# Plain fp32 on four column strips in place of split fp32r products, in the expert layer of a two-layer decoder trunk

## The reference, cut to what matters

```
D_MODEL, SEQ, N_EXPERTS, TOP_K_EXPERTS, D_FF_EXPERT = 1024, 256, 8, 2, 3584
def swiglu(h, w1, w3, w2):
    return (jax.nn.silu(h @ w1) * (h @ w3)) @ w2
def moe_ffn(h, router_w, w1, w3, w2):
    logits = (h @ router_w).astype(jnp.float32)
    vals, idx = lax.top_k(logits, TOP_K_EXPERTS)
    probs = jax.nn.softmax(vals, axis=-1)
    gate = jnp.sum(jax.nn.one_hot(idx, N_EXPERTS) * probs[..., None], axis=-2)
    out = jnp.zeros_like(h)
    for e in range(N_EXPERTS):
        out = out + gate[..., e:e + 1] * swiglu(h, w1[e], w3[e], w2[e])
    return out
```

## Time and profile before

| | |
|---|---|
| three runs | 1673.94, 1678.23, 1680.12 us; median 1678.23 us |
| the profiled execution | 1676.77 us, of which the span from first to last instruction is 1675.0 us |
| mean granted PE clock | 0.993 |
| busy share of the span | PE 98%, PEld 83%, DVE 81%, ACT 64%, POOL 27% |
| moved by DMA | 481.57 MB, of them 336 transfers of 1024 KB of expert weights |

### The profile page before, as it was taken

How to read it: one execution, slowest core, us unless ns; L and a number is a source line. 1 busy time by engine, 2 the same in 40 slices (tenths; PEclk the granted TensorE clock), 3 DMA queues, 4 the chain that set the end, 5 groups by cost and what they waited for, 6 DMA issues and landing times.

```text
span 1675.0 us, 24200 instructions
## 1 busy us (share of the span) xinstructions
PE 1641.8 (98%) x8916; PEld 1384.0 (83%) x8916; DVE 1363.3 (81%) x1134; ACT 1064.2 (64%) x894; POOL 444.8 (27%) x541
## 2 busy tenths in 40 slices
PE   8999999999999999999999999999999999999998
PEld 5887888999888788878888888888888888888886
DVE  5799675556669876688888988888888988888888
ACT  4345456444455544577777777777777777777775
POOL 8966802999152341233000000000000000000200
PEclk9999999999999999999999999999999999999999
DMA  8443556556445355389999999999999999999995
GB/s 294 158 158 115 175 189 217 181 190 219 150 152 176 126 176 185 121 314 396 384 381 388 365 384 385 367 386 385 369 387 382 372 384 377 379 383 370 391 395 195
DMA packets 212459, 481.57 MB, mean 287 GB/s; under 512 B 7936, under 2 KB 32640, under 8 KB 212144
## 3 DMA queue, kind: packets, MB, share of 16 engines
q1 hardware_dynamic: 207456, 463.34, 76.8%
q0 software_dynamic: 4512, 16.78, 2.7%
q10 hardware_dynamic: 432, 0.65, 0.1%
HBM read 473.40 MB, written 7.34 MB: 287 GB/s over the span
## 4 chain that ended last, share of the span: by engine, by line
PE 67%; DVE 2%; ACT 1%; issue 0%; DVEq 0%; ACTq 0%
PE ps L655 20%; PE ps L657 20%; PE ps L656 20%; PE ps L1330 1%; PE ps L701 1%; PE ps L703 1%; PE ps L702 1%; DVE w_lo L286 1%; PE ps L891 0%; PE ps L1406 0%; PE ps L1283 0%; ACT w_hi L280 0%; PE ps L1387 0%; DVE keybias L2171 0%; DVE keybias L2169 0%
## 5 line engine op out<-in xcount | busy, mean ns | idle before, releaser
L286 DVE TENSOR_TENSOR w_lo<-raw,w_hi 128x2048 fp32r<-128x2048 f32 (+1 forms) x433 | 1005.9, 2326 | 220.6 <-ACT w_hi L280 219.1
L280 ACT ACTIVATE w_hi<-raw 128x2048 fp32r<-128x2048 f32 (+1 forms) x433 | 830.0, 1918 | 410.1 <-PE ps L657 323.0
L655 PE MATMUL ps<-w_hi,xg_hi 128*128 128x512 f32 x896 | 354.5, 396 | 1.2 <-DVE w_lo L286 1.2
L657 PE MATMUL ps<-w_hi,xg_lo 128*128 128x512 f32 x896 | 349.5, 390 | 0.0
L656 PE MATMUL ps<-w_lo,xg_hi 128*128 128x512 f32 x896 | 349.0, 390 | 0.0
L655 PE MATMUL ps<-w_hi,hidT_hi 128*128 128x512 f32 x520 | 203.2, 391 | 0.0
L656 PE MATMUL ps<-w_lo,hidT_hi 128*128 128x512 f32 x520 | 202.5, 389 | 0.0
L657 PE MATMUL ps<-w_hi,hidT_lo 128*128 128x512 f32 x520 | 202.4, 389 | 0.0
L657 PEld LDWEIGHTS ps<-w_hi,xg_lo 128*128 128x128 f32 x896 | 168.2, 188 | 35.8
L655 PEld LDWEIGHTS ps<-w_hi,xg_hi 128*128 128x128 f32 x896 | 168.3, 188 | 35.4 <-DVE w_lo L286 1.7
L656 PEld LDWEIGHTS ps<-w_lo,xg_hi 128*128 128x128 f32 x896 | 168.5, 188 | 33.4
(11 more groups left out here) (432 smaller groups left out, 2409.5 us busy)
## 6 DMA issues: line engine op xcount, KB each, us to landing
raw<-moe_w SPq DMA_DIRECT2D x336, 1024.0 KB, 6.2
raw<-w_in SPq DMA_DIRECT2D x44, 1024.0 KB, 5.5
raw<-ffn_w SPq DMA_DIRECT2D x33, 1024.0 KB, 5.4
raw<-w_o SPq DMA_DIRECT2D x8, 1024.0 KB, 5.0
raw<-w_out_a SPq DMA_DIRECT2D x4, 1024.0 KB, 5.3
raw<-w_out_c SPq DMA_DIRECT2D x4, 1024.0 KB, 5.2
raw<-w_out_b SPq DMA_DIRECT2D x4, 1024.0 KB, 5.1
raw<-w_in SPq DMA_DIRECT2D x4, 904.0 KB, 7.4
```

The lines of the kernel that those rows point to most:

```text
L280: act.activation(w_hi[:, n % SPLIT, 0:width], raw[:, n % RAW, 0:width], ACT.Copy)\
L286: dve.tensor_tensor(w_lo[:, n % SPLIT, 0:width], raw[:, n % RAW, 0:width], w_hi[:, n % SPLIT, 0:width].bitcast(F32), ALU.subtract)\
L655: pe.matmul(dst, x_hi, hi, start=first, stop=False, skip_group_check=True)
L657: return pe.matmul(dst, x_lo, hi, start=False, stop=last, skip_group_check=True)
```

## The change

The expert layer and the router stop splitting. The experts multiply the raw chunks in plain fp32. `SLOTS` falls from 128 to 96 (up to three rounds would be made for fuller experts; the fullest has 71 tokens). The 96 slots are three strips of 32; each strip multiplies the first 384 of the 512 weight columns (`wide`). The fourth strip takes the last 128 columns for all three groups of slots, one after another (`narrow`), the first of them issued ahead of the three wide ones. A hidden block is therefore stored as 96 rows by 384 columns and, on partitions 96 to 127, three pieces of 32 rows by 128 columns; only three transposes turn it. ACT's and DVE's splits of the 336 chunks go, SP's loads wait for `used` in place of `lo_done`, the turned hidden block is one copy on DVE, ACT's copy of an expert's rows takes four instructions, and the last expert's rows are put together by further copies. The router multiplies fp32 rows with fp32 weights, one product where there were three. The first gather runs once in fp32 in place of once for each part. The variance in a norm loses one DVE instruction (ACT's square root takes scale and bias).

```diff
-SLOTS = P
+SLOTS = 96
+ROUNDS = -(-SEQ // SLOTS)
+TILE = 32
+TILES = SLOTS // TILE
 NEG = -1e30
 DEAD = -3e38
 HALF = 512
+WIDE = HALF * TILES // 4
...
-            def load_at(n, turns, src):
+            def load_at(n, turns, src, read=lo_done):
 
                 free = value(sp, n - RAW + 1 + 6 * turns)
-                sp.wait_ge(lo_done, free)
+                sp.wait_ge(read, free)
                 shape = tuple(src.shape[1:])
...
@@ -602,12 +622,12 @@
                     col = value(sp, t * HALF)
                     for half in range(2):
                         row = value(sp, KD * e + 4 * half)
-                        load_at(m + half, turns, w[:, bass.ds(row, 4), bass.ds(col, HALF)])
+                        load_at(m + half, turns, w[:, bass.ds(row, 4), bass.ds(col, HALF)], used)
 
                 def down(m, turns, e, t):
                     for half in range(2):
                         row = value(sp, K2 * e + 4 * t + 2 * half)
-                        load_at(m + half, turns, w2e[:, bass.ds(row, 2), :])
+                        load_at(m + half, turns, w2e[:, bass.ds(row, 2), :], used)
...
                 def logits_of(b):
 
-                    tok = slice(b * P, b * P + P)
                     dst = ps[:, 0, b * EXPERTS:(b + 1) * EXPERTS]
                     for k in range(KD):
+                        tok = slice(k * P, k * P + P)
                         if k % 4 == 0:
-                            pe.wait_ge(S["hT_lo_done"], 12 + 2 * b + k // 4 + 1)
-                        pe.matmul(dst, hT_hi[:, k, tok], router_hi[:, k, :], start=b == 0 and k == 0, stop=False,
-                                  skip_group_check=True)
-                        pe.matmul(dst, hT_hi[:, k, tok], router_lo[:, k, :], start=False, stop=False,
-                                  skip_group_check=True)
-                        mm = pe.matmul(dst, hT_lo[:, k, tok], router_hi[:, k, :], start=False, stop=k == KD - 1,
-                                       skip_group_check=True)
+                            pe.wait_ge(S["hT_hi_done"], 12 + 2 * b + k // 4 + 1)
+                        mm = pe.matmul(dst, y_back[:, b, 0, tok], router_sb[:, k, :], start=b == 0 and k == 0,
+                                       stop=k == KD - 1, skip_group_check=True)
                     return mm
 
                 def stay_awake(times):
...
+                def loaded(m, turns):
+
+                    pe.wait_ge(raw_full[m % RAW], 16 * (m // RAW + 1) + 16 * turns)
+
+                def four_tiles(bank, x_of, w, first, last):
+
+                    def wide(g):
+                        pe.matmul(ps[tile_rows(g), bank, 0:WIDE], x_of(g), w[:, 0:WIDE], start=first, stop=last,
+                                  skip_group_check=True, tile_position=(0, TILE * g))
+
+                    def narrow(g):
+                        return pe.matmul(ps[SLOTS:P, bank, g * P:(g + 1) * P], x_of(g), w[:, WIDE:HALF],
+                                         start=first and g == 0, stop=last, skip_group_check=True,
+                                         tile_position=(0, SLOTS))
+
+                    narrow(0)
+                    for g in range(TILES):
+                        wide(g)
+                    narrow(1)
+                    return narrow(2)
+
+                def hidden_tile(t, c):
+
+                    return lambda g: (t[:, c * P + TILE * g:c * P + TILE * g + TILE] if c < TILES else
+                                      t[:, g * P + SLOTS:(g + 1) * P])
 
                 def up(n, which, i, turns, other_half=False):
 
@@ -1314,52 +1355,48 @@
                     for half in range(2):
                         m = n + half
                         if half == 1 and other_half:
-                            pe.wait_ge(S["xg_hi_done"], 1)
-                            pe.wait_ge(S["xg_lo_done"], 1)
-                        pe.wait_ge(lo_done, m + 1 + 6 * turns)
+                            pe.wait_ge(S["xg_second"], 1)
+                        loaded(m, turns)
                         for k in range(4):
                             kk = 4 * half + k
-                            mm = three(ps[:, which, :], xg_hi[:, kk, :], xg_lo[:, kk, :], m,
-                                       lambda w: slot_view(w, m, (4, HALF))[:, k, :], kk == 0, kk == KD - 1)
+                            mm = four_tiles(which, lambda g: xgT[:, kk, tile_rows(g)],
+                                            slot_view(raw, m, (4, HALF))[:, k, :], kk == 0, kk == KD - 1)
                         mm.then_inc(used, 1)
 
                 def turn_hidden(i):
 
                     pe.wait_ge(S["hid_done"], i + 1)
-                    for k in range(4):
+                    for k in range(TILES):
                         tr = pe.transpose(ps[:, 4, k * P:k * P + P], hid[:, k * P:k * P + P], ident[:, :])
                     tr.then_inc(S["hidT_ps"], 1)
 
...
                 def down(n, i, turns, first=False, middle=None):
 
-                    pe.wait_ge(S["hidT_lo_done"], i)
+                    pe.wait_ge(S["hidT_copied"], i - DENSE_STRIPES)
+                    for chunk in range(2):
+                        m = n + chunk
+                        loaded(m, turns)
+                        for k in range(2):
+                            for half in range(2):
+                                mm = four_tiles(2 + half, hidden_tile(hidT, 2 * chunk + k),
+                                                slot_view(raw, m, (2, D))[:, k, half * HALF:(half + 1) * HALF],
+                                                first and chunk == 0 and k == 0, False)
+                            if middle is not None and chunk == 0 and k == 0:
+                                middle()
+                        mm.then_inc(used, 1)
+
+                def last_down(n, i, turns):
+
...
+                    if rnd == 0:
+                        pe.wait_ge(S["h_rows_made"], BLOCKS)
+                    for k in range(KD):
+                        for b in range(BLOCKS):
+                            mm = pe.matmul(ps[:, 6 + k // 4, (k % 4) * P:(k % 4) * P + SLOTS],
+                                           h_all[:, b, k * P:k * P + P], pick[:, b, :],
+                                           start=k % 4 == 0 and b == 0, stop=b == 1, skip_group_check=True)
+                        if k % 4 == 3:
+                            mm.then_inc(S["gather_ps"], 1)
...
+            def turned_x(b, halves):
+
+                for half in halves:
+                    act.wait_ge(S["hT_ps"], 12 + 2 * b + half + 1)
+                    act.activation(y_back[:, b, 0, half * HALF:(half + 1) * HALF], ps[:, 4 + 2 * b + half, :], ACT.Copy)\
+                       .then_inc(S["hT_hi_done"], 1)
...
-                def stripe(i, t, turns, begun=False):
-
-                    if not begun:
-                        split_hi(act, n0 + 6, turns)
-                    split_hi(act, n0 + 7, turns)
-                    split_hi(act, n0 + 8, turns)
-                    hidden_hi(i + t - 1, 4)
-                    silu(i + t, n0 + 6 + 6 * turns)
-                    split_hi(act, n0 + 9, turns)
+                def xg(e):
+                    act.wait_ge(S["gather_ps"], 2 * (e0 + e) + 1)
+                    act.activation(xgT[:, 0:4, :], quarters(ps[:, 6, :])[:, :, 0:SLOTS], ACT.Copy)\
+                       .then_inc(S["xg_first"], 1)
+
+                def up(i, t, turns):
+                    silu(i + t, n0 + 6 + 6 * turns, WIDE)
+
+                def rows_out(e):
+
+                    act.wait_ge(S["rows_stored"], 16 * e + 16)
+                    rows = y_sb[:, :].rearrange("s (h n) -> s h n", h=2)
+                    act.activation(rows[:, :, 0:WIDE], ps[0:SLOTS, 2:4, 0:WIDE], ACT.Copy).then_inc(S["y_taken"], 1)
+                    for g in range(TILES):
+                        act.activation(rows[tile_rows(g), :, WIDE:HALF], ps[SLOTS:P, 2:4, g * P:(g + 1) * P],
+                                       ACT.Copy).then_inc(S["y_taken"], 1)
+
+                def y(e, half):
+
+                    at = half * HALF
+                    moved = value(act, 6 * scattered_before(rnd, e) + 3 * half + 3)
+                    act.activation(y_hi[:, at:at + WIDE], ps[0:SLOTS, 2 + half, 0:WIDE], ACT.Copy)\
+                       .then_inc(S["y_hi_done"], 1)
+                    for g in range(TILES):
+                        act.activation(y_sb[tile_rows(g), at + WIDE:at + HALF],
+                                       ps[SLOTS:P, 2 + half, g * P:(g + 1) * P], ACT.Copy)\
+                           .then_inc(S["y_moved"], 1)
+                    act.wait_ge(S["y_moved"], moved)
+                    act.activation(y_hi[:, at + WIDE:at + HALF], y_sb[:, at + WIDE:at + HALF], ACT.Copy)\
+                       .then_inc(S["y_hi_done"], 1)
 
                 def expert(e, last):
...
+                def hidden(seen, dst=hidT):
+                    dve.wait_ge(S["hidT_ps"], seen)
```

(68 more changed lines are left out.)

325 lines of the change are left out of this document (107 added, 218 removed).

## The result

The changed kernel takes 1715.43 us (median of four runs, 1712.14 to 1716.29) against 1678.65 us before: a ratio of 1.022, 95% interval 1.0196 to 1.0245. It is slower by 37 us where 32 us less were forecast, and it lies outside the range. Its profiled execution took 1716.29 us, span 1714.5, mean clock 0.972.

The account below looks back on a forecast made before the run. PE's pace was taken to bound the expert layer. From 1676.8 us, 26 us in the layer and 6 in its head gave 1644.8, set at 1646 us because the profiled execution ran 1.5 us under the median; range 1626 to 1670 us.

Parts of the forecast that it names:

- The step that failed: Expert layer, first to last transposes: 54.5 stripes gain 0.51 us each, less 0.2 us for seven experts: 26 us gained.
- The k step and the stripe: Expert layer on PE: the narrow strip sets a k step of 0.656 us; a stripe takes 16.28 us against 16.79.
- the sum for transposes and two switches: Each stripe: three transposes cost 0.34 us, two switches between strips and whole array 0.20 us.
- the 6 us of the forecast: Head of the layer, router to first transposes: router blocks, gather and first k steps together gain 6 us.
- The gather: Head of the layer: one fp32 gather in place of two parts takes 2.4 us, 1.3 us less.
- The 24 k steps: Head, after the gather: 24 k steps and a switch take 15.85 us against 18.27, 2.4 us less.
- The tail: End of the kernel: PE's vanished wait and added moves and copy for the last rows cancel within 1 us.
- The spare of the transfers: Expert layer loads: an expert needs 391 GB/s, 409 were seen, so PE stays the bound with 4% to spare.
- Wide products that hold narrow ones: Rival, strips: narrow products may not end before earlier wide ones; k step 0.865 us, 281 us more, 1927 us; chance 0.11.
- The transfers as the bound at 385 GB/s: Rival, expert layer: an expert takes 117.4 us, 14 us of the gain goes, 1660 us; chance 0.13.
- A gain eaten on PE: Rival: four moving operands read at once make a k step 0.675 us, giving 26 us back, 1672 us; chance 0.08.
- The wide row decides: Rival: the wide strips set the pace, k step 0.646 us, 13 us less, 1633 us; chance 0.12.

Follow-up runs that it names:

- experiment 1: Changed kernel with PE's loop over the first seven experts written out, same products in the same order: 1644.97 us (four runs), ratio 0.9802.
- 10: Changed kernel with all seven stripes of an expert as one inner loop, differences picked by branches (42 KiB body): 1649.18 us, ratio 0.9837.
- 11: Changed kernel with an expert's stripes as one inner loop, but the last stripe written out behind it (79 KiB body): 1644.76 us, one run.
- 4: Kernel before with its inner loop over stripes written out and two experts in a pass (141 KiB body): 1693.72 us, one run.
- 9: Kernel before with two experts in a pass, inner loops kept (102 KiB body): 1693.39 us (two runs), ratio 1.0082.
- 5: Changed kernel, expert loop written out, first narrow product issued after the three wide ones instead of ahead: 1645.88 us, one run.
- experiment 6: Changed kernel, expert loop written out, second and third narrow product of each k step left out: 1635.53 us, one run.
- experiment 7: Changed kernel, expert loop written out, one narrow product and wide ones of 256 columns instead of 384: 1642.23 us, one run.

## Why the prediction was wrong

**The step that failed.** It is "From the first transposes at 731.42 to the last stripe's at 1656.78 there are 54 stripes and a half one: 54.5 x 0.51 - 7 x 0.2 = **26 us** gained." It counts what PE executes, and lets nothing stand between one expert and the next. No rival had it either: all of them were about strips, transfers and data. The change multiplies the program that one pass of the loop holds by 3.6, from 51 to 184 KiB, and somewhere between 79 and 102 KiB the head of the body is no longer there when PE jumps back to it. In place of 26 us gained, that stretch lost 41.6: six jumps cost 69.4 us, 58 of them waiting and 11 behind the gaps, and the rest gained 27.8. This is shown from both sides: the changed kernel without the stalls (experiments 1, 10, 11), the kernel before with them (4, 9).

The count could have been made from the code. The trace of before had half of the hint: its code queue has 38 packets in all and none from 842 to 1578 us, so the loop's code was being kept. The other half is a rule of the Trainium skill, page "Runtime: NRT & Kernel Launch", section "Instruction fetch mechanics": PE's instruction memory holds 128 KiB, is refilled in blocks of 16 KiB while it runs, and a taken branch to code outside a window of two blocks has to fetch it first. The traces agree on the 16 KB packets, on the free straight run and on the stall at a jump. They differ on the window: 79 KiB back cost nothing here, which is more than two blocks, and 102 KiB did stall, which is less than 128.

**The k step and the stripe were right.** 0.656 us came from the narrow strip, and experiments 5 and 6 show that it decides: the wide strips alone would be 9 ns faster (forecast 10). A stripe was put at 16.28 and is 16.32 us; the sum for transposes and two switches was 0.54 us and is 16.32 - 24 x 0.656 = 0.58.

**The sum without the stalls was right.** The 79 KiB case has a span of 1643.0 us, 32.0 under before. Its first transposes come at 724.70 (6.7 us earlier; forecast 6), its last at 1623.88 (899.2 us between them against 925.4: 26.2 gained; forecast 26), and the end 19.1 us later (0.9 lost; forecast nothing, within 1). The middle agrees by a compensation that nobody forecast: the stripes of the token search gained 0.66 us and those of the gathered rows 0.47, more than taken, and the start of the last expert lost some 2.5 us. In the changed kernel's own profile the transposes come only 3.3 us earlier, because that execution reached the router 2.7 us later (699.58 against 696.88), where the 79 KiB case reached it 0.7 us earlier with the same code up to there.

From the router to the first transposes both take 28.5 us against 34.5 before: the 6 us of the forecast, but partly by luck. The gather was put at 2.4 us and took 3.64 (3.72 before), since PE issues both its halves, 32 records, ahead of `up`; this term gained 0.1 us in place of 1.3. What lies between the router and the gather made up for it, with 3.5 us gained where some 2.5 were counted. The 24 k steps behind them gained the 2.4 us forecast.

**The tail**: ACT's three moves took 0.86 us together and its further copy 0.31, DVE's second product 0.29. The end lost 1.1 us (0.9 in the 79 KiB case), where nothing was counted.

**The spare of the transfers was wrong.** "PE stays the bound with 4% to spare" took 409 GB/s from 11 us just after the head. Under experiment 7 the layer holds 389 to 392. An expert at the new pace needs 391, so the spare is nothing: from the first to the last transposes experiment 7 takes 899.6 us with a quarter of PE's work gone, and the 79 KiB case 899.2 with all of it. It did no harm because the need falls exactly on the limit: experiment 6 asked for 113.9 us an expert and got 115.0 to 115.3, the first experiment asks for 115.4 and gets it.

**The rivals.** Wide products that hold narrow ones: refuted, narrow records follow one another 0.109 us apart past the wide ones issued before them, and stripes are 16.3 us, not 21. The transfers as the bound at 385 GB/s: not reached, but nearer than its 0.13 said. A gain eaten on PE: no, reading four operands at once costs nothing that can be seen. The wide row decides: no. The forecast said that a clock below 1.00 would break it; it fell, but as a result of the gaps.

**Open.** Why a stall is 10 us in the changed kernel and 6.5 in the other: it would fit if PE still had products in hand when the code ran out, of 0.23 us in the one and of 0.11 in the other, but no run shows it. The limit between 79 and 102 KiB was not narrowed. At the start of the last expert all versions without the stalls lose 2 to 4 us. In the 79 KiB case these are pauses of PE of 0.3 to 0.7 us between 1538 and 1541 us, for which the profile names no data; only experiments 1 and 5 show a wait for weights there (0.5 and 1.6 us). Beside them SP, leaving its loop, issues one transfer late (waits of 3.6 us in experiment 1, 4.9 with 79 KiB). Which of it is the cause was not tried.

## What to carry to other kernels

When an edit turns one instruction into several inside a loop, count the bytes of that engine's loop body as well as its time. Here 79 KiB of PE's program looped at no cost, and from 102 KiB on every jump back cost 8 to 13 us; the cures are to write the loop out (1645 us) or to fold its copies until it fits (1645 us with 79 KiB), while a body that is merely smaller gives nothing back. Take the rate that transfers can hold from a stretch as long as the one you plan for, not from a burst.

## What was unexpected on the chip

- A jump back to code that has to be fetched: 6.3 to 6.8 us idle with 102 and 141 KiB in the kernel before, 9.3 to 10.5 us with 112, 184 and 368 KiB in the changed one. The size beyond the limit does not matter.
- Behind gaps of 6.3 us and more the clock was at the lower of its two levels: eight or more products start 0.427 us apart in place of 0.227. In the changed kernel the record of half clock is 10.2 us long at five gaps and 13.7 at one.
- Products of 128 and 384 columns on four strips run beside one another without a loss that can be seen: 0.109 us a record on the narrow strip, and 0.323 on each wide one where the wide strips set the pace (experiment 6), and the order of issue is worth 1 ns a k step.
